# Gate and up slabs in shared block products: seven products of both pairs instead of seven of the gate and two plain units of up

## What is computed

```
def swiglu(h, w_gate, w_up, w_down):
    return (jax.nn.silu(h @ w_gate) * (h @ w_up)) @ w_down
...
h = modulate(rms_norm(x, norm_ffn1[i]), sh1, sc1)
x = x + 0.5 * gt1[:, None, :] * swiglu(h, ffn1_gate[i], ffn1_up[i], ffn1_down[i])
...
h = modulate(rms_norm(x, norm_ffn2[i]), sh3, sc3)
x = x + 0.5 * gt3[:, None, :] * swiglu(h, ffn2_gate[i], ffn2_up[i], ffn2_down[i])
```

## Time and profile before

| | |
|---|---|
| median of 3 runs | 1434.01 us (1432.2 to 1434.07) |
| span of the profiled execution, first to last instruction | 1432.1 us |
| PE busy | 1389.1 us, 97% |
| DVE busy | 977.2 us, 68% |
| ACT busy | 539.3 us, 38% |
| DMA | 189.49 MB, mean 132 GB/s |

### The profile page before, as it was taken

One profiled execution on the slowest core, in us unless ns is written; L12 is line 12 of the kernel. 1 busy time (PEld: TensorE's weight loads), 2 busy tenths in 40 slices (PEclk: granted clock), 3 DMA queues, 4 the chain that ended last, 5 costly groups with the idle time before them and its releaser, 6 DMA issues.

```text
span 1432.1 us, 28796 instructions
## 1 busy us (share of the span) xinstructions
PE 1389.1 (97%) x11782; PEld 1344.0 (94%) x11782; DVE 977.2 (68%) x1731; ACT 539.3 (38%) x797; POOL 80.2 (6%) x120
## 2 busy tenths in 40 slices
PE   6999999999999999999999999999999999999996
PEld 5899999999998999999899897999899999999996
DVE  6446675357547588998998997854554776456745
ACT  5423343224336222524243237422352344224433
POOL 6100000010001000000000000100000000000000
PEclk9999999999999999999999999999999999999998
DMA  9754646454364223213334453626312332323321
GB/s 322 237 177 155 205 149 206 147 168 142 103 208 142 89 88 93 89 60 104 125 128 146 136 169 127 220 91 198 104 59 74 92 117 89 114 76 106 101 77 60
DMA packets 132701, 189.49 MB, mean 132 GB/s; under 512 B 4621, under 2 KB 112545, under 8 KB 132386
## 3 DMA queue, kind: packets, MB, share of 16 engines
q1 hardware_dynamic: 111388, 112.54, 25.0%
q0 software_dynamic: 17136, 66.87, 14.0%
q10 hardware_dynamic: 4070, 8.57, 1.6%
HBM read 173.73 MB, written 15.18 MB: 132 GB/s over the span
## 4 chain that ended last, share of the span: by engine, by line
PE 84%; DVE 10%; ACT 3%; issue 2%; DMA 1%; POOL 0%; DVEq 0%; ACTq 0%
PE pu L646 51%; PE pu L828 13%; PE pu L817 11%; PE pu L660 2%; PE pg L690 2%; DVE w_lo L1680 1%; DMA work<-in_w_ada 1%; PE pg L1064 1%; ACT w_hi L1227 1%; DVE d L2106 1%; DVE w_lo L1969 1%; DVE work L2216 1%; PE pg L726 0%; DVE work L2215 0%; DVE work L2227 0%
## 5 line engine op out<-in xcount | busy, mean ns | idle before, releaser
L1680 DVE TENSOR_TENSOR w_lo<-raw,w_hi 128x1024 fp32r<-128x1024 f32 x152 | 186.1, 1225 | 255.5 <-ACT w_hi L1227 255.4
L1227 ACT CAST w_hi<-raw 128x1024 fp32r<-128x1024 f32 x152 | 158.9, 1046 | 412.0 <-PE pu L646 373.0
L646 PE MATMUL pu<-h_hi,w_hi 128*128 128x260 f32 x1408 | 288.4, 286 | 4.6 <-DVE work L2381 2.8
L646 PE MATMUL pu<-h_hi,w_lo 128*128 128x260 f32 x1408 | 284.1, 283 | 0.0
L646 PE MATMUL pu<-h_lo,w_hi 128*128 128x260 f32 x1408 | 283.3, 283 | 0.0
L646 PEld LDWEIGHTS pu<-h_hi,w_hi 128*128 128x128 f32 x1408 | 217.7, 189 | 8.7 <-DVE w_lo L1680 4.8
L646 PEld LDWEIGHTS pu<-h_hi,w_lo 128*128 128x128 f32 x1408 | 217.4, 189 | 0.0
L646 PEld LDWEIGHTS pu<-h_lo,w_hi 128*128 128x128 f32 x1408 | 217.2, 189 | 0.0
L2106 DVE SCALAR_TENSOR_TENSOR d<-u,cw,d 128x512 f32<-128x512 f32 x240 | 163.2, 745 | 0.1
L646 PE MATMUL pu<-f_hi,w_hi 128*128 128x260 f32 x704 | 142.9, 284 | 0.0
L646 PE MATMUL pu<-f_hi,w_lo 128*128 128x260 f32 x704 | 141.8, 283 | 0.0
(11 more groups left out here) (352 smaller groups left out, 2369.7 us busy)
## 6 DMA issues: line engine op xcount, KB each, us to landing
raw_a<-in_w_ada POOLq DMA_DIRECT2D x30, 1024.0 KB, 7.9
raw<-in_w_in SPq DMA_DIRECT2D x28, 1024.0 KB, 5.2
raw<-in_ffn_up SPq DMA_DIRECT2D x22, 1024.0 KB, 5.3
raw<-in_ffn_gate SPq DMA_DIRECT2D x21, 1024.0 KB, 5.3
raw<-in_ffn_down SPq DMA_DIRECT2D x16, 1024.0 KB, 5.1
gates_d<-sg ACTq DMA_DIRECT2D x24, 260.0 KB, 2.4
raw<-in_ffn_down SPq DMA_DIRECT2D x8, 768.0 KB, 4.4
work<-gates_d POOLq DMA_DIRECT2D x2, 2080.0 KB, 8.8
```

What stands on the lines that cost most here:

```text
L646: last = mm(pu[p][:, e, 0:HALF], w[p][:, k, :], m[:, k, e * HALF:(e + 1) * HALF], start=(k == 0 and j == 0), stop=(k == k_tiles - 1 and j ...
L1227: nc.scalar.copy(w_hi[p][:], raw[:, slot, :, p * P:(p + 1) * P]).then_inc(s_hi, 1)
L1680: V.tensor_tensor(w_lo[p][:], raw[:, slot, :, p * P:(p + 1) * P], w_hi[p][:].bitcast(F32), ALU.subtract).then_inc(s_lo, 1)
```

## The change

Each of the seven block products now works on both slabs: `product` takes `half` (0 gate, 1 up), and every position issues 12 matmuls for gate and 12 for up, with the same activation block. The plain up units are gone, so a turn is 7 x 24 = 168 matmuls. `TURN` becomes 7 and the order P1, P2, P5, P6, P7, P4, P3.

A weight block now holds both slabs, 128 x 1024, which fills all of `w_hi[p]`; the two buffers alternate, so ACT and DVE make the block two positions ahead. The sums of weight blocks become 128 x 1024 as well, and are spread over the turn: one each at P1 and P5 for this turn, one each at P6 and P3 for the next.

P6, P7 and P4 are accumulated in PSUM on top of P1 (`start=False`), P3 on top of P5. ACT copies P1, P1+P6 and P1+P6+P7 out of PSUM (`s_p1`, `s_u2`, `s_u3`), the last two by halves, gate while up is still being multiplied. DVE makes three additions of both pairs, 128 x (2 x 260). P1 sits in `pu[0]`, P2 in `pu[1]`, P5 in two banks of `pg`.

Silu, multiplication and split of a turn's row 1 come at P4 and P3, those of row 0 at P3 of the turn and P1 and P2 of the next; `f_lo` of row 1 at P7 of the next. In the last turn of a group all of them come at P3, and the first down unit takes its last two k tiles in swapped order (row 0 last).

The slabs are loaded in four DMAs of 512 KB per turn: the upper 512 rows of gate and up once the sum for P6 is made, the lower 512 rows once P4's low part is. The down slabs of a group (slots 0 and 1) are both loaded after P4's low part. The loads of the convolution state on POOL move behind the turns of the first stage, since `w_sums` has grown over their place. The conditioning tiles are made after P1 instead of P4, in PSUM banks 0 and 1 of `pg`; two semaphores of the spill of `x` rows become one. The core of the diff, removed lines mostly left out:

```
-TURN = 11
+TURN = 7
 TURNS = 4
-P1, P2, P6, P5, P7, P4, P3, U0A, U0B, U1A, U1B = range(TURN)
+P1, P2, P5, P6, P7, P4, P3 = range(TURN)
 SUM_OF = {P5: 0, P6: 1, P7: 2, P3: 3}
+SUM_COUNT = {P7: 1, P5: 2, P6: 3, P3: 4}
...
+                    def rows_of(it, k2, sem):
+                        for slot, w in enumerate((wg, wu)):
+                            if it == 0 and k2 == 0:
+                                sp.wait_ge(s_lo, n0 - 2 + 2 * slot)
+                            c = r0 + 256 * it
+                            sp.dma_start(raw[:, slot, 4 * k2:4 * k2 + 4, :], cols(w, c, 4, 4 * k2 * P)).then_inc(sem, 16)
                     for it, t in turns(which, g):
-                        if it == 0:
-                            sp.wait_ge(s_lo, n0 - 2)
-                        else:
+                        if it:
+                            sp.wait_ge(s_wsum, 4 * (t - 1) + SUM_COUNT[P6])
+                        rows_of(it, 0, s_raw0)
+                        if it:
                             sp.wait_ge(s_blo, TURN * (t - 1) + P4 + 1)
-                        sp.dma_start(raw[:, 0], cols(wg, r0 + 256 * it)).then_inc(s_graw, 16)
-                        if it == 0:
-                            sp.wait_ge(s_lo, n0)
-                        else:
-                            sp.wait_ge(s_blo, TURN * t)
-                        sp.dma_start(raw[:, 1], cols(wu, r0 + 256 * it)).then_inc(s_uraw, 16)
+                        rows_of(it, 1, s_raw1)
                     sp.wait_ge(s_blo, TURN * t + P4 + 1)
                     load(Lin(n0), 0, cols(wd, 0, r0=r0))
-                    sp.wait_ge(s_blo, TURN * (t + 1))
                     load(Lin(n0 + 2), 1, cols(wd, 256, r0=r0))
...
+            def product(j, bank, half, hi, lo, start=True):
...
+                        last = mm(bank, w_blocks(w, j)[:, half, k, :], m[:, k, :],
+                                  start=(start and k == 0 and n == 0), stop=(k == 3 and n == 2),
+                                  skip_group_check=not start)
+                return last
...
                 for it, t in turns(which, g):
                     j = TURN * t
+                    a, b, c = pu[0][:, :, 0:HALF], pu[1][:, :, 0:HALF], pg[:, 2:4, 0:HALF]
...
+                        pe.wait_ge(s_um, 3 * t - 2)
+                    pe.wait_ge(s_blo, j + P1 + 1)
+                    for e in range(2):
+                        last = product(j + P1, a[:, e], e, h_block(h_hi, 0, 0), h_block(h_lo, 0, 0))
+                    last.then_inc(s_bd, 1)
+                    if m < LATE0:
+                        ada(Lin(m))
+                        ada(Lin(m + 1))
...
+                        pe.wait_ge(s_c12, t)
+                    pe.wait_ge(s_blo, j + P5 + 1)
+                    for e in range(2):
+                        last = product(j + P5, c[:, e], e, t_hi[:, 0], t_lo[:, 0])
+                    last.then_inc(s_bd, 1)
                     pe.wait_ge(s_p1, t + 1)
+                    pe.wait_ge(s_blo, j + P6 + 1)
+                    product(j + P6, a[:, 0], 0, t_hi[:, 1], t_lo[:, 1], start=False).then_inc(s_gh, 1)
+                    product(j + P6, a[:, 1], 1, t_hi[:, 1], t_lo[:, 1], start=False).then_inc(s_bd, 1)
+                    pe.wait_ge(s_blo, j + P7 + 1)
+                    pe.wait_ge(s_u2, 2 * t + 1)
+                    product(j + P7, a[:, 0], 0, t_hi[:, 2], t_lo[:, 2], start=False).then_inc(s_gh, 1)
+                    pe.wait_ge(s_u2, 2 * t + 2)
...
+                    product(j + P7, a[:, 1], 1, t_hi[:, 2], t_lo[:, 2], start=False).then_inc(s_bd, 1)
                     if m < LATE0:
                         ada_transpose(Lin(m))
                         ada_transpose(Lin(m + 1))
+                    pe.wait_ge(s_blo, j + P4 + 1)
+                    pe.wait_ge(s_u3, 2 * t + 1)
+                    product(j + P4, a[:, 0], 0, t_hi[:, 3], t_lo[:, 3], start=False)
+                    pe.wait_ge(s_u3, 2 * t + 2)
+                    product(j + P4, a[:, 1], 1, t_hi[:, 3], t_lo[:, 3], start=False).then_inc(s_bd, 1)
+                    pe.wait_ge(s_c22, t + 1)
+                    pe.wait_ge(s_blo, j + P3 + 1)
+                    for e in range(2):
+                        last = product(j + P3, c[:, e], e, h_block(h_hi, 1, 1), h_block(h_lo, 1, 1), start=False)
+                    last.then_inc(s_bd, 1)
...
+            def blocks_hi(t, pos):
                 if pos in SUM_OF:
...
+                gate, up = sg[:, 2:4, :], lb[:, 2:4, :]
+                def hidden_hi(t, it, row, um):
+                    act.wait_ge(s_um, 3 * t + um)
+                    nc.scalar.copy(f_hi[:, 2 * it + row, :], gate[:, row, :]).then_inc(s_ahi, 1)
                 for it, t in turns(which, g):
+                    last = it + 1 == TURNS
                     for pos in range(TURN):
+                        if pos in (P6, P7):
+                            act.wait_ge(s_gh, 2 * t + 1 + (pos == P7))
+                            if pos == P7:
+                                act.wait_ge(s_c11, t + 1)
+                            row, s_read = (1, s_u2) if pos == P6 else (0, s_u3)
+                            nc.scalar.copy(sg[:, row, 0:HALF], pu[0][:, 0, 0:HALF]).then_inc(s_read, 1)
                         act.wait_ge(s_bd, TURN * t + pos + 1)
+                        if pos in (P6, P7):
+                            nc.scalar.copy(sg[:, row, HALF:N], pu[0][:, 1, 0:HALF]).then_inc(s_read, 1)
+                        if pos + 2 < TURN:
+                            blocks_hi(t, pos + 2)
+                        elif not last:
+                            blocks_hi(t + 1, pos + 2 - TURN)
+                        else:
+                            k = pos - P4
+                            split_hi(Lin(at[f"down{which}_{g}"] + k), k, 0)
                         if pos == P1:
+                            nc.scalar.copy(halves(sg[:, 0, :]), psum(0)).then_inc(s_p1, 1)
+                            if it:
+                                hidden_hi(t - 1, it - 1, 0, 3)
+                        if pos == P2:
+                            ada_part(0, ADA_UP[g] + 2 * it, None)
+                        if pos == P4:
+                            act.wait_ge(s_c22, t + 1)
+                            af(gate[:, 1, 0:HALF], pu[0][:, 0, 0:HALF], ACT.Silu).then_inc(s_sg, 1)
+                            af(gate[:, 1, HALF:N], gate[:, 1, HALF:N], ACT.Silu).then_inc(s_sg, 1)
                         if pos == P3:
+                            hidden_hi(t, it, 1, 2)
                             act.wait_ge(s_c12, t + 1)
+                            af(gate[:, 0, :], gate[:, 0, :], ACT.Silu).then_inc(s_sg, 1)
+                            if last:
+                                hidden_hi(t, it, 0, 3)
...
+            def add_weights(t, pos):
+                s1, s2, s3, s4 = (w_sums[:, SUM_OF[p]] for p in (P5, P6, P7, P3))
+                out, a, b, op = {P7: (s3, raw_blocks(0, 0), raw_blocks(1, 0), ALU.subtract),
+                                 P5: (s1, raw_blocks(1, 0), raw_blocks(1, 1), ALU.add),
+                                 P6: (s2, s1, raw_blocks(0, 0), ALU.subtract),
+                                 P3: (s4, raw_blocks(0, 1), s2, ALU.subtract)}[pos]
+                if pos == P7:
+                    dve.wait_ge(s_raw0, 32 * (t + 1))
+                if pos == P5:
+                    dve.wait_ge(s_raw1, 32 * (t + 1))
+                dve.wait_ge(s_wsum, 4 * t + SUM_COUNT[pos] - 1)
+                if t:
+                    dve.wait_ge(s_blo, TURN * (t - 1) + pos + 1)
                 V.tensor_tensor(out, a, b, op).then_inc(s_wsum, 1)
...
+                def hidden_lo(t, it, row, count):
+                    dve.wait_ge(s_ahi, a1 + count)
+                    V.tensor_tensor(f_lo[:, 2 * it + row, :], gate[:, row, :], f_hi[:, 2 * it + row, :].bitcast(F32),
+                                    ALU.subtract).then_inc(s_a, 1)
+                def multiplied_row0(t):
+                    dve.wait_ge(s_sg, 3 * t + 3)
+                    V.tensor_tensor(gate[:, 0, :], gate[:, 0, :], up[:, 0, :], ALU.mult).then_inc(s_um, 1)
                 for it, t in turns(which, g):
                     last = it + 1 == TURNS
                     for pos in range(TURN):
                         dve.wait_ge(s_bd, TURN * t + pos + 1)
+                        if pos == P1:
+                            add_weights(t, P6)
+                        if pos == P2 and it:
+                            hidden_lo(t - 1, it - 1, 0, 2 * it)
+                        if pos == P5:
+                            add_weights(t, P3)
+                        if pos == P7:
+                            if it:
+                                hidden_lo(t - 1, it - 1, 1, 2 * it)
+                            dve.wait_ge(s_u3, 2 * t + 2)
+                            if it:
+                                dve.wait_ge(s_a, HIDDEN0 + a1 + 2 * it)
+                            V.tensor_tensor(gate_up[:, :, 3, HALF:N], halves(sg[:, 0, :]), pair_c, ALU.add
```

(62 more changed lines are left out.)

203 lines of the change are left out of this document (55 added, 148 removed).

## The result

The changed kernel takes 1463.53 us (median of 4 runs, 1461.96 to 1464.39) against 1433.99 before: a ratio of 1.0208, with an interval from 1.0194 to 1.0223.

What follows compares the result with a forecast made beforehand. PE's matmuls bound the kernel, with hardly a stall to remove. PE work -22.7, old stalls -2.0, stalls in turns +22.1, group ends +21.3 give +18.6 on 1432.1 = 1450.7, plus 1.9 for the median: 1452.6 us; range 1429 to 1468.

Steps and rivals of the forecast that it cites:

- Matmuls, -22.7: 12 of 180 matmuls removed in each turn, 1.42 us less; 22.7 us over 16 turns.
- The turn, 22.2: A steady turn takes 22.2 us against 21.58 before, with stalls at four places.
- (c): At P6 and P7 ACT first copies half a pair: 0.11 us of stall.
- (a): At P3 DVE's late addition holds up ACT's silu of row 0, so P5's w_hi starts late: 0.52 us stall.
- (a) to (d): Four stalls in a steady turn: 0.52 us ahead of P5, 0.68 ahead of P6, 0.11, 0.75 ahead of P3; together 2.06.
- Groups: The four groups of turns should take 98.0, 95.1, 93.2 and 92.3 us.
- the bound that was given: At group ends, a down slab landing at 6.6 us instead of 5.2 costs 5.6 us.
- Ends, 21.3: First down unit waits for the seventh tile's f_lo: 5.2 us in each group, 5.75 in the first; 21.3 us.
- The clock: Rival: clock falls at group ends, 1.8 us lost each, four times 7 in all: 1459.6 us; chance 0.16.
- Late loads: Rival: 512 KB halves following one another land at 7.4 us, 1457.9; landing at 8 gives 1463.5; chance 0.12.
- Conversions hide: Rival: real chain short enough that stalls in turns vanish, only ends of groups remain: 1430.5 us; chance 0.12.

Runs made afterwards that it cites:

- fewer_mm: Kernel before the change, with the last two k tiles of U1B left out, 12 matmuls fewer a turn: 1408.66 us, ratio 0.9831.
- order_late_sum: Changed kernel, ACT and DVE work reordered inside the turn, DVE's sum for the next P7 behind P3's low part: 1445.36 us, ratio 1.0077.
- six_tiles: Changed kernel with one number changed: a group's first down unit starts when six hidden tiles are there, not seven: 1449.11 us, ratio 1.0107.
- tail: Changed kernel with new group ends: upper down-slab halves loaded earlier, last turn's work reordered, first down unit starting at six tiles: 1437.48 us, ratio 1.0026.
- order_and_tail_old_loads: order_and_tail with the down slabs loaded as in the changed kernel, one 1 MB DMA each when P4's low part is made: 1427.03 us, ratio 0.9952.
- filler: Changed kernel plus 36 unread matmuls on PE in the wait at each group's end: 1456.69 us, ratio 1.0166.
- order_and_tail: Order inside the turns from order_late_sum and group ends from tail, together: 1419.56 us, ratio 0.9894.
- order: Changed kernel, ACT and DVE work reordered inside the turn, DVE's sum for the next P7 ahead of P4's low part: 1458.89 us, ratio 1.0173.
- order_small_cond: Kernel of order with POOL's conditioning loads up to the turns' end cut from 1 MB to 128 KB each: 1443.92 us, ratio 1.0073.
- order_filler: Kernel of order_late_sum plus 36 unread matmuls in the wait at each group's end: 1438.62 us, ratio 1.0036.

## Why the prediction was right, and where it was short

The direction and the mechanism held, and the measured 1463.5 lies in the range, 10.9 above the forecast of 1452.6. By its steps:

- **Matmuls, -22.7.** Held: 1.43 us a turn in fewer_mm, 22.9 in all.
- **The turn, 22.2.** Held: 22.32, and 23.2 to 23.9 with conditioning tiles, where 23.2 was forecast. PE's gaps beyond its pitch in the steady turn were 0.45 ahead of P5 (forecast 0.52), 0.53 ahead of P6 (0.68), 0.05 for (c) (0.11) and 0.77 ahead of P3 (0.75), 1.80 together; each was followed by another 0.08 to 0.11 ahead of the second matmul, which makes the 2.16 us above 20.16. The order of (a) shows as it was laid out: ACT stands idle for 1.44 us until DVE's addition lets it start the silu at 1349.24, and the cast for P5 follows at 1349.78. That the stalls come from the order of ACT's and DVE's work, as (a) to (d) say, and not from its amount, is shown by order_late_sum, which does the same work in steady turns of 20.48 us, and in 87.7 and 87.5 us for the last two groups where the changed kernel takes 93.2 and 92.6.
- **Groups.** Forecast 98.0, 95.1, 93.2, 92.3; measured 99.4, 96.9, 93.2, 92.6. The two of the second stage are right to 0.3. The two of the first are 3.2 us short together, of which 1.9 are their ends and 1.3 their turns. In group 1 the conditioning loads were put at nothing, "5 us earlier in a turn", and so was SP's request of the upper rows. Each may be nothing by itself; but the change had put them within 2 us of each other (160.65 and 162.27), the rows landed 8.8 and 10.9 us after the request, and 0.5 to 1.1 us were lost a turn ahead of P3 alone, where 0.5 was forecast for all of it. Inside the turns this is the step that failed: an edit was costed at nothing by the time to its first use, with the landing time of a quiet queue. In group 2 the down slab came after 6.7 us instead of 5.2, inside the bound that was given, and the wait was 6.8.
- **Ends, 21.3.** Held: 6.1, 6.8, 5.2 and 5.2 us, 23.3 in all; without the late slab of group 2 and the late start of group 1, 5.2 each. That f_lo of the seventh tile is what PE waits for stands in the list of waits, and six_tiles, tail and order_and_tail_old_loads each take a part of it away.
- **The clock.** Named as the first rival, with a chance of 0.16, and it came true in full: 7 us, as worked out from 1.8 a piece (measured 1.74 in the chain, 1.7 with filler). That it was put at nothing in the sum is the largest single miss. The row for it, 1.94 us idle near the start, stood against windows with 1.3 us idle in pieces; a wait of 5.2 us lies beyond both, on the side of the row that fell. The trace of the kernel before had a better row than either: at 924.15, amid dense matmuls, a wait of 1.98 us with 1.2 GHz behind it. With it the clock belonged in the forecast, 1459.6, and not among the rivals. The Trainium skill's rule on idle gaps between bursts (TensorE: Matmul & The Clock Gate, HAM oscillation) was the better guide here, and the traces agree with it at every end with over 5 us of idle.
- **The other rivals.** Late loads had the right place (group 1) but the wrong cause: not the halves following one another, whose medians were 4.0 and 5.0 us, but a neighbour's 2 MB. That its price at 8 us, 1463.5, equals the measured time is chance. "Conversions hide" fell as argued.

In sum: 18.6 forecast, +7.0 clock, +3.5 in the groups (2.0 at the ends, 1.4 in the turns), makes 29.1; the span grew by 28.3, since the fall at 924.7 was in the kernel before alone.

So the saving wasn't absent, it was spent twice over. The turns alone, at 20.16 us and 2.54 for each of the five with conditioning tiles, would take 335.3; the groups took 382.1, of which 23.3 are the ends and 23.5 the turns, and the clock took 7.0 behind them. In order_and_tail, with the same matmuls and conversions, the groups take 8.9 us more than that 335.3: 2.8 are the ends, the rest lies in turns of 20.48 instead of 20.16 and in the first turns of groups. Whether these can be had too was not tried.

## What to carry to other kernels

When a change halves the buffering ahead of the busiest engine, write down for every position what the feeding engines do between the release and the block that is due, and put there only what the block needs. All else goes behind it; the amount of work was the same in 1463 and in 1420 us. An instruction that waits for a load belongs as late as its own user allows, since it holds up everything queued behind it, and a load's landing has to be costed together with what other queues ask for in the same microseconds. And a wait of TensorE can cost more than its length, in these traces always from 3 us on and sometimes at 2: look at the matmuls behind it, not only at the gap.

## What the runs showed of the hardware

- **The clock falls behind a single wait in dense work.** After 5.2 to 6.8 us idle it was at 1.2 GHz at every end of the changed kernel and came back 3.4 to 4.5 us after PE resumed. After 0.5 to 1.6 us idle it stayed at 2.4 GHz at the ends of tail and order_and_tail. The three stalls of 2.7 to 3.4 us in group 1 of order each had a fall behind them, and so had the 3.7 us at the second end of six_tiles and of order_and_tail_old_loads. No trace has a wait of 3 us or more in dense work without a fall.
- **Around 2 to 3 us the idle time alone doesn't tell.** The clearest case is one wait that all 13 traces of this document have, 2.1 us long, the one at 924.15 in the kernel before (row above): the clock fell behind it in 7 of them and stayed in 6, the changed kernel's among the latter. At the ends, in six_tiles it fell with 2.4 us and stayed with 2.6 and 2.7; in order_and_tail_old_loads it stayed at one end with 2.0 us, fell at another with 2.0, and at the fourth, with 2.4, it fell some 1.3 us after PE was back. Behind the useless matmuls it stayed with 2.5 us in filler and fell with 2.1 in order_filler. What decides in this middle range stays open.
- **Useless matmuls in a wait pay for themselves.** 144 of them, 36 x 0.12 = 4.3 us at each end, made the kernel 6.8 us faster, and 6.7 us in a second kernel, although they don't protect every end.
- **A landing time is not a property of a load.** The same pair of 512 KB halves landed in 4.2 and 5.2 us beside two loads of 128 KB (order_small_cond), and in 8.8 and 10.9 us beside two of 1 MB on another queue (order).
